# Two chained blocks on one core: the opening's vectors shared by two engines, one stream of modulation steps, sums of squares added up ahead

## The reference

```python
# first block, per layer l (mod = silu(c) @ ada_w[l] + ada_b[l], nine vectors of 1024)
n1 = rms_norm(h, norm_g[l, 0]) * (1 + sc1) + sh1
h = h + 0.5 * g1 * swiglu(n1, ...)          # F0 / F2
h = h + g2 * token_mixing(n2, ...)          # two attentions, gates, out
h = h + 0.5 * g3 * swiglu(n3, ...)          # F1 / F3
return rms_norm(h, final_g)
# second block, streams x and ctx (xc); per layer sh1, sc1, g1, sh2, sc2, g2 = silu(c) @ w_mod[i] + b_mod[i],
# and the same for c_ctx; layer 0 mixes by retention and gated linear scans, layer 1 by attention
yc, states = retention_gla_mixer(hc, ...)
y, _ = retention_gla_mixer(h, ..., states)
x = layer_norm(ALPHA * x + g1 * (y @ w_out), ...)
x = layer_norm(ALPHA * x + g2 * sq_relu_mlp(x * (1 + sc2) + sh2, w1, w2), ...)
```

## Time and profile before

| | us |
|---|---|
| median of 3 runs | 2336.91 (2334.52 to 2337.52) |
| profiled execution | 2339.74 |
| its span | 2338.0 |
| TensorE busy (matmul) | 2243.5 |
| VectorE, ScalarE, GpSimd busy | 1759.6, 1158.2, 109.5 |
| mean granted TensorE clock | 0.984 of full |

### The profile page before, as it was taken

One profiled execution on the slowest core, in us unless ns is written; L12 is line 12 of the kernel. 1 busy time (PEld: TensorE's weight loads), 2 busy tenths in 40 slices (PEclk: granted clock), 3 DMA queues, 4 the chain that ended last, 5 costly groups with the idle time before them and its releaser, 6 DMA issues.

```text
span 2338.0 us, 34014 instructions
## 1 busy us (share of the span) xinstructions
PE 2243.5 (96%) x14388; PEld 1960.2 (84%) x14404; DVE 1759.6 (75%) x2083; ACT 1158.2 (50%) x1445; POOL 109.5 (5%) x157
## 2 busy tenths in 40 slices
PE   7999999999999999999999889899989998999998
PEld 6888899888888888988888779778878887768886
DVE  3788776788888878678886666668788877676763
ACT  2544556555355445655534434447536633475742
POOL 1000000000000000000000000000000000000000
PEclk7999999999999999999999999999999999999999
DMA  6988664488878866448887426239788876304651
GB/s 242 311 278 305 228 198 145 148 298 291 307 228 276 306 223 210 140 145 291 288 305 246 137 80 204 100 109 293 261 278 276 269 277 225 109 19 140 203 197 55
DMA packets 330447, 505.24 MB, mean 216 GB/s; under 512 B 12327, under 2 KB 239878, under 8 KB 330295
## 3 DMA queue, kind: packets, MB, share of 16 engines
q1 hardware_dynamic: 288071, 340.70, 44.2%
q0 software_dynamic: 41616, 160.44, 19.7%
q10 hardware_dynamic: 608, 1.92, 0.2%
HBM read 501.98 MB, written 1.05 MB: 215 GB/s over the span
## 4 chain that ended last, share of the span: by engine, by line
PE 85%; DVE 9%; ACT 3%; issue 2%; DMA 1%; POOL 0%; ACTq 0%; DVEq 0%; SPq 0%; POOLq 0%
PE banks L577 35%; PE banks L578 18%; PE banks L569 7%; PE banks L571 7%; PE banks L570 7%; PE banks L796 2%; PE banks L743 2%; DVE wlo L1761 1%; PE banks L770 1%; PE banks L826 1%; PE banks L779 1%; PE banks L634 1%; DVE arena L1788 1%; DMA stage<-in_ffn_wu_dram 1%; DMA arena<-in_ada_w_dram 1%
## 5 line engine op out<-in xcount | busy, mean ns | idle before, releaser
L1761 DVE TENSOR_TENSOR wlo<-stage,whi 128x2048 fp32r<-128x2048 f32 (+1 forms) x326 | 737.1, 2262 | 184.2 <-ACT whi L1290 183.2
L1290 ACT CAST whi<-stage 128x2048 fp32r<-128x2048 f32 x322 | 615.0, 1911 | 387.7 <-PE banks L578 304.0
L577 PE MATMUL banks<-xs,whi 128*128 128x512 f32 x2176 | 768.0, 398 | 7.8 <-DVE xs L2008 4.3
L578 PE MATMUL banks<-xs,wlo 128*128 128x256 f32 x2176 | 609.5, 280 | 0.0
L577 PEld LDWEIGHTS banks<-xs,whi 128*128 128x128 f32 x2176 | 409.0, 188 | 109.0 <-issue 5.1
L569 PE MATMUL banks<-xs,whi 128*128 128x256 f32 x1440 | 416.5, 289 | 11.9 <-DVE xs L1952 7.9
L578 PEld LDWEIGHTS banks<-xs,wlo 128*128 128x128 f32 x2176 | 411.2, 189 | 0.1
L570 PE MATMUL banks<-xs,whi 128*128 128x256 f32 x1440 | 408.4, 284 | 0.0
L571 PE MATMUL banks<-xs,wlo 128*128 128x256 f32 x1440 | 408.3, 284 | 0.0
L577 PE MATMUL banks<-hidden_arena,whi 128*128 128x512 f32 x992 | 357.6, 402 | 1.1 <-DVE wlo L1761 1.1
L1788 DVE SCALAR_TENSOR_TENSOR arena<-modw,cact,arena 128x1024 f32<-128x1024 f32 x234 | 299.8, 1281 | 23.3 <-DMA modw<-in_w_mod_dram 15.7
(11 more groups left out here) (329 smaller groups left out, 2489.9 us busy)
## 6 DMA issues: line engine op xcount, KB each, us to landing
stage<-in_mlp_w_dram SPq DMA_DIRECT2D x96, 1024.0 KB, 5.4
modw<-in_w_mod_dram POOLq DMA_DIRECT2D x80, 1024.0 KB, 5.9
modw<-in_ada_w_dram POOLq DMA_DIRECT2D x66, 1024.0 KB, 5.5
stage<-in_ffn_wg_dram SPq DMA_DIRECT2D x44, 1024.0 KB, 5.7
stage<-in_ffn_wu_dram SPq DMA_DIRECT2D x44, 1024.0 KB, 7.3
stage<-in_ffn_wd_dram SPq DMA_DIRECT2D x44, 1024.0 KB, 7.4
stage<-in_ev_w_in_dram SPq DMA_DIRECT2D x24, 1024.0 KB, 5.4
stage<-in_w_in_dram SPq DMA_DIRECT2D x18, 1024.0 KB, 5.7
```

What stands on the lines that cost most here:

```text
L577: mm(out, hi, pair.rearrange("p a t -> p (a t)"), start=first_mm, stop=False, skip_group_check=True)
L578: return mm(out[:, 0:T], lo, pair[:, 0, :], start=False, stop=last_mm, skip_group_check=True)
L1290: nc.scalar.copy(whi[:, s, :], stage[:, s, :]).then_inc(hi_done, 1)
L1761: last = v.tensor_tensor(wlo[:, s, at], stage[:, s, at], whi[:, s, at].bitcast(F32), ALU.subtract)
```

## The change

It has five parts.

1. *Opening.* Of every quarter of the first scale and the first shift vector, VectorE takes the even half (`first_steps`: four steps a vector) and TensorE the odd half (`column_step`: eight one-column matmuls); `column_rest` adds VectorE's accumulator with eight more into the same column. No turn is left here. The first norm is done by rows: ScalarE squares x in rows with a running sum, VectorE multiplies the rows by the root, TensorE transposes them once more (`turn_rows("normal")`), and VectorE takes them from PSUM with the scale. The column sums n0 are gone. `keep_warm` calls of 4 or 2 stand between the groups.
2. *One stream of steps.* A vector may end in another phase than it began. Steps go into gate0 and gate1 (8 each), evoc and evox (4 each) and 4 more into evx; F1 and F3 have 32 for 40, Mc and M0 34 for 40. `ACC_ROOMS` holds five accumulators; a step waits only for the turn of the vector that last used its own. The vectors of the gate phases are turned at w = 1 of F1 and F3; in evc and evx a turn comes one chunk after the last step.
3. *Joined sums.* In evc and evx VectorE adds the 8 blocks up to one (`join`), and TensorE sums it in one matmul, for the squares of n6 and lc0 and the mean of lc0. Root and finish come one or two chunks later; in Mc and M0 the layer norm's pieces come one chunk later.
4. *Scan.* Three buffers for the query, the third in `xs`; `decays(u)` waits for the outputs of u - 3. The `keep_warm` calls inside the loop are gone, and two more memsets stand ahead of it.
5. The small transfers of evc are issued one load later.

```diff
-            "start": [ada(0, 1)],
             "F0": [ada(0, v) for v in range(2, 6)],
             "in0": [ada(0, 6), ada(0, 7)],
-            "F1": [ada(0, 8)] + [ada(1, v) for v in range(4)],
+            "gate0": [ada(0, 8)],
+            "F1": [ada(1, v) for v in range(4)],
             "F2": [ada(1, 4), ada(1, 5), wmod(0, 0, 2), wmod(0, 1, 2)],
             "in1": [ada(1, 6), ada(1, 7)],
-            "F3": [ada(1, 8), wmod(0, 2, 2)] + [wmod(0, v, 1) for v in range(3)],
-            "evc": [wmod(0, 3, 2), wmod(0, 4, 2)],
-            "evx": [wmod(0, 3, 1)],
-            "Mc": [wmod(0, 5, 2), wmod(0, 4, 1), wmod(0, 5, 1), wmod(1, 0, 2), wmod(1, 1, 2)],
-            "M0": [wmod(1, v, 1) for v in range(5)],
+            "gate1": [ada(1, 8)],
+            "F3": [wmod(0, 2, 2)] + [wmod(0, v, 1) for v in range(3)],
+            "evc": [wmod(0, 3, 2), wmod(0, 4, 2), wmod(0, 5, 2), wmod(0, 3, 1), wmod(0, 4, 1)],
+            "Mc": [wmod(0, 5, 1), wmod(1, 0, 2), wmod(1, 1, 2), wmod(1, 0, 1)],
+            "M0": [wmod(1, v, 1) for v in range(1, 5)],
...
+        gate_vectors = (mod_first["gate0"], mod_first["gate1"])
+        ACC_ROOMS = {"arena": arena[:, 43 * 256:47 * 256], "low": plain_rows[:, 0:1024], "mid": plain_rows[:, 1024:2048],
+                     "top": plain_rows[:, 2048:3072], "table": table[:]}
+
+        def acc_name(m):
+            if m in gate_vectors:
+                return "top"
+            if even0 <= m < even0 + 4:
+                return ("low", "mid")[(m - even0) % 2]
+            return "table" if m == even0 + 4 else "arena"
+
+        macc_of = lambda m: ACC_ROOMS[acc_name(m)]
+        acc_before = lambda m: max([a for a in range(m) if acc_name(a) == acc_name(m)], default=None)
+        first_acc = (ACC_ROOMS["arena"], hid[:].rearrange("p s f t -> p (s f t)")[:, 0:1024])
...
         STEPS = {
             "F0": [0] + 22 * [1] + 4 * [2] + [0, 0, 1, 1, 0, 0],
-            "F1": [0] + 4 * [1, 1, 1, 2] + 6 * [1] + 4 * [2] + [2, 0, 2, 2, 0, 0],
-            "Mc": [0] + 3 * [1, 1, 2, 1, 1] + [1, 0, 2, 2, 0, 2, 2, 2, 0, 2, 2, 0, 2, 2, 3, 0],
+            "in0": [2, 2, 2, 2, 0, 1, 1, 3, 3],
+            "gate0": [2, 1, 1, 1, 1, 1, 1],
+            "evc": [2, 2, 2, 0, 1, 1, 2, 2, 2, 2, 0, 0],
+            "evoc": [1, 2, 1, 0],
+            "evx": [1, 1, 0, 1, 1, 2, 0, 2, 2, 2, 0, 0],
+            "evox": [1, 2, 1, 0],
+            "Mc": [0] + 3 * [1, 1, 1, 1, 2] + [1, 0, 1, 2, 0, 2, 2, 2, 0, 2, 1, 0, 1, 2, 0, 0],
             "M1": [0, 0] + 8 * [1] + 22 * [0],
         }
-        for name, like in (("F2", "F0"), ("F3", "F1"), ("M0", "Mc")):
+        for name, like in (("F1", "F0"), ("F2", "F0"), ("F3", "F0"), ("in1", "in0"), ("gate1", "gate0"), ("M0", "Mc")):
...
+        turn_at["F1", 1], turn_at["F3", 1] = gate_vectors
+        EVEN_TURNS = {"c": {6: even0, 10: even0 + 1}, "x": {7: even0 + 2, 10: even0 + 3}}
...
-            "qd": [part(16 + 2 * i, 2) for i in range(2)],
+            "qd": [part(16, 2), part(18, 2), plain_xs[:, KB - 2:KB, :]],
...
-        EVEN_TURNS = {"c": (5, 9), "x": (9,)}
-        EVEN_STEPS = {"c": (1, 2, 2, 0, 2, 1, 2, 2, 2, 2, 0, 0), "x": (1, 1, 0, 1, 1, 0, 1, 1, 1, 1, 0, 0)}
+        JOIN_AT = {"c": 2, "x": 4}
...
-                if c == RING:
+                if c == RING + 1:
...
+            def column_step(i, q):
+
+                pe.wait_ge(start_landed[4 * i + q], 16)
+                t = 2 * q + 1
+                for k in range(KB):
+                    mm(first_column[i][:, k:k + 1], quarter(4 * i + q)[:, 1024 + k * P:1024 + (k + 1) * P], cact[:, 0, t:t + 1],
+                       start=q == 0 and k == 0, stop=False, skip_group_check=True)
+
+            def column_rest(i):
+
+                pe.wait_ge(first_step[i], 4)
+                for k in range(KB):
+                    last = mm(first_column[i][:, k:k + 1], first_acc[i][:, k * P:(k + 1) * P], ones[:, 0:1],
+                              start=False, stop=True, skip_group_check=True)
+                last.then_inc(pe_out.sem, pe_out.next(f"column{i}"))
+
             keep_warm(Y[:, 3, :], 12)
+            pe.wait_ge(act_out.sem, act_out.at("cact"))
+            column_step(0, 0)
+            keep_warm(R[:, 0, :], 4)
             turn_rows(0)
+            column_step(0, 1)
+            keep_warm(R[:, 0, :], 4)
             pe.wait_ge(param_landed, nparam)
             for k in range(KB):
                 transpose(R[:, 1, k * nwide:(k + 1) * nwide], wide_room[:, k * P:(k + 1) * P], nwide)
             transpose(R[:, 1, KB * nwide:KB * nwide + 7], narrow_room, 7).then_inc(pe_out.sem, pe_out.next("params"))
-            pe.wait_ge(act_out.sem, act_out.at("cact"))
-            turn_mod(0, R[:, 2:4, :])
-            rms_stat("n0")
+            for q in (2, 3):
+                column_step(0, q)
+                keep_warm(R[:, 0, :], 2)
+            column_rest(0)
+            pe.wait_ge(dve_out.sem, dve_out.at("rows"))
             pe.wait_ge(act_out.sem, act_out.at(("turned", 0)))
-            for t in range(8):
-                if t % 2 == 0:
-                    pe.wait_ge(start_landed[4 + t // 2], 16)
-                for k in range(KB):
-                    last = mm(Y[:, 0, k:k + 1], quarter(4 + t // 2)[:, (t % 2) * 1024 + k * P:(t % 2) * 1024 + (k + 1) * P],
-                              cact[:, 0, t:t + 1], start=t == 0 and k == 0, stop=t == 7, skip_group_check=True)
-            last.then_inc(pe_out.sem, pe_out.next("shift0"))
-            keep_warm(Y[:, 1, :], 12)
+            turn_rows("normal")
+            for q in range(4):
+                column_step(1, q)
+                keep_warm(R[:, 0, :], 2)
+            column_rest(1)
+            keep_warm(R[:, 0, :], 4)
...
-                    if which == "c" and c == 1:
-                        column_sums(other)
                     if which == "x" and c == 1:
-                        mean_sums(other, other_res)
-                    if which == "x" and c == 3:
-                        column_sums(other)
-                    if c == EVEN_TURNS[which][0]:
+                        pe.wait_ge(dve_out.sem, dve_out.at((other, "joined mean")))
+                        mm(stats_of(other)[3], ones, stats_of(other)[0][:, 0, :], start=True, stop=True) \
+                            .then_inc(pe_out.sem, pe_out.next((other, "mean")))
+                    if c == min(EVEN_TURNS[which]):
                         pe.wait_ge(dve_out.sem, dve_out.at((other, "rooted")))
                     if c in EVEN_TURNS[which]:
-                        turn_mod(mod_first["ev" + which] + EVEN_TURNS[which].index(c), Y[:, 2:4, :])
+                        turn_mod(EVEN_TURNS[which][c], Y[:, 2:4, :])
...
-                    if u < 3:
-                        keep_warm(R[:, 0, :], 3)
                     if u >= 1:
                         outputs(u - 1)
                     states(u)
...
+            def first_steps(i, q):
+
+                dve.wait_ge(start_landed[4 * i + q], 16)
+                w, cc = quarter(4 * i + q)[:, 0:1024], cact[:, 0, 2 * q:2 * q + 1]
+                if q == 0:
+                    v.tensor_scalar(first_acc[i], w, cc, None, ALU.mult).then_inc(first_step[i], 1)
+                else:
+                    dve.wait_ge(first_step[i], q)
+                    v.scalar_tensor_tensor(out=first_acc[i], in0=w, scalar=cc, in1=first_acc[i], op0=ALU.mult, op1=ALU.add) \
+                        .then_inc(first_step[i], 1)
...
+            for q in range(4):
+                first_steps(0, q)
+            dve.wait_ge(act_out.sem, act_out.at("rows"))
+            refine(row_rs, row_room, row_sum, D, 1e-6)
+            dve.wait_ge(pe_out.sem, pe_out.at(("turned", 0)))
+            for a in range(2):
+                last = v.tensor_scalar(xrows[:, a, :], xrows[:, a, :], row_rs[:, a:a + 1], None, ALU.mult)
+            done(last, "rows")
...
+                    mod_steps(STEPS[f"gate{l}"][g])
...
+            def join(key, signal_name, src):
+
+                room = stats_of(key)[0]
+                link(v.tensor_tensor(room[:, 0:4, :], src[:, 0:4, :], src[:, 4:8, :], ALU.add))
+                link(v.tensor_tensor(room[:, 0:2, :], room[:, 0:2, :], room[:, 2:4, :], ALU.add))
+                done(v.tensor_tensor(room[:, 0, :], room[:, 0, :], room[:, 1, :], ALU.add), (key, signal_name))
...
-                    if u >= 2:
-                        dve.wait_ge(pe_out.sem, pe_out.at(("o", which, u - 2)))
+                    if u >= 3:
+                        dve.wait_ge(pe_out.sem, pe_out.at(("o", which, u - 3)))
...
+            def first_shift():
+                first_steps(1, 2)
+                first_steps(1, 3)
+                conv(0)
+                first_vector(1)
+                done(v.memset(stat[:, 61:62], 0.0), "start_shift")
+
+            dve.wait_ge(pe_out.sem, pe_out.at(("turned", "normal")))
+            normal_split("n0", "F0", resx, lambda k: mc(("ada", 0, 0), k), first_shift)
```

155 lines of the change are left out of this document (84 added, 71 removed).

## The result

The changed kernel takes 2314.53 us, the median of four executions (2312.03 to 2318.83); the kernel before takes 2335.88 us, the median of four. The ratio is 0.9907, with a 95% interval of 0.9896 to 0.9919: faster by 21.4 us. The forecast was 2298, with a range of 2280 to 2314. The side is right, the gain is little more than half of the 38.7 us forecast, and the time lies just above the range. The profiled execution of the changed kernel took 2312.03 us for a span of 2310.2 us, 27.8 us less than the span before.

The account below looks back on a forecast made before the run. TensorE, busy in 96% of the span, was taken as the bound. Opening +1, ends of Mc and M0 -17.3, even projections -17.0 and scans -5.4 made -38.7: 2301.0 from the profiled 2339.7, 2298 by the median; range 2280 to 2314.

Parts of the forecast that it names:

- The second rival: Outside the opening: new waits eat half of the 39.7 us gain, giving 2318 us; chance 13%.
- if TensorE waits for the joined sums: evc and evx: a sign, named in advance, that the prediction is wrong; no size given.
- Ends of Mc and M0: Fewer steps behind the modulated input, no turn there in Mc, 0.5 us wait left in M0: -17.3 us.
- Even projections: Even mixer's projections, evc and evx: turns without waits and joined sums save 17.0 us (ends -10 and -18.3).
- up to 1.1, 0.8 taken: evx, joined sum at c = 4: TensorE's wait in us behind cast, low part and adds.
- each turn comes one chunk behind its last step: evc: the two turns no longer wait or run slowly, -7.2 us.
- Scans: -2.7 each: Both scans: three short waits and three warm-up groups on the chain go, together -5.4 us.
- Opening: +1: Opening: column work shared with TensorE, partly at the lower clock, costs net 1 us (ends -13.5 and +12).
- The fall near 23 us: Opening: TensorE's clock stays full to about 23 us, then runs at 1.2 GHz.
- the full-clock rival: Opening stays at full clock, 14.5 us further down, 2284 us; chance 22%.
- The third rival: Moved steps wait for their weight transfers; above 2.8 us unhidden each, slower than before; wholly unhidden 2381 us; chance 3%.
- the fourth: Rival: TensorE's turns move but wait as long, only removed matmuls pay: 2324 us; chance 4%.

Follow-up runs that it names:

- e4_three: Changed kernel with one Mc step moved a window later, evc's final norm and evx's join each moved ahead of a low part: 2294.11 us.
- s1_scans: e4_three with both scans put back as in the kernel before: 2301.5 us.
- a_again: The changed kernel itself, unedited, timed again: 2312.33 us.
- o2b_six: e4_three with six warm-up matmuls instead of two behind each of the opening's last six column quarters, repeated for a profile: 2289.79 us, single execution.

## Why the prediction was wrong

**The second rival came true in part.** It had 13% and said that each stage which loses a stall meets the next limit. It gave 2318; measured were 2314.5. It took half of the 39.7 us outside the opening away; in the profiled executions 22.8 of them came. The opening, 6 us better than forecast there, hid a part of the miss: that is luck and not the forecast's reasoning. The stages with the three new waits taken out come near the forecast's terms: Mc 9.7 us (2.4 and 7.3; forecast 8.8), evc 9.2 (5.1 and 4.1; 9.9), evx 5.0 (5.9), M0, which never had such a wait, 9.7 (8.5). The sizes of what was removed were about right. The step that failed is where the new order's waits were costed: 0 for Mc's turns, 0 for the norm in evc, 0.8 us for the join in evx. Taking them out gave 7.3, 4.1 and 7.4 us. The prediction had named one of these as a sign of being wrong, "if TensorE waits for the joined sums", and TensorE did.

**Ends of Mc and M0: "Mc has no turn there any more".** True and not enough. The count of steps was followed only behind the modulated input. With 34 steps in the new order Mc's fourth turn falls in window 23, the last whose turn lies in the banks of the second half, and its take-out falls in the next window behind the residual. M0 has the same table but begins at another step of a vector, its turn falls in window 22, and nothing waits. A term for the turns of the whole phase, with the banks of each, would have shown the wait: 5.42 us and 1.4 of slow matmuls.

**Even projections: a wait of "up to 1.1, 0.8 taken".** The join stands behind a cast, a low part and the adds, as the forecast had it; but ahead of the cast ScalarE does three activations from 1411.62 to 1414.83. They were in the trace of before, where nobody waited for them. The wait was 4.57 us, and with the slow matmuls behind it, for which the forecast had no term, the stage lost 7.4 us. For evc, "each turn comes one chunk behind its last step" left out that the final norm moved from c = 3 to c = 4, in front of that step: 2.31 us waited, 4.1 for the stage. The later turns also put the take-out of the last turn ahead of the scans, where TensorE now waits 1.4 us instead of 0.72 in each; that is still so in e4_three, and no run takes it out.

**Scans: -2.7 each.** Another term that was too large. Measured 1.1 and 0.7 against before, and 1.6 each by undoing. Units 1 to 2 and 2 to 3 came 0.55 and 1.05 us closer, units 3 to 4 and 5 to 6 not at all, which is the pattern forecast. But the first wait grew by 0.82 us (2.10 to 2.92), for the memsets (in s1_scans, without them, the longest wait is 2.2 again), and the matmuls removed had mostly filled waits.

**Opening: +1, found -5.0.** The fall near 23 us was right, 0.53 at 24 to 28, and the full-clock rival (22%) is out for this kernel. (One reading of the trace was loose and cost nothing: before, TensorE did not stand idle from 13.0 to 23.9 us, since 25 transposes of 2.75 us lie in between the earlier trace rows.) Three parts were off. The column groups at 34.12 and 36.42 took 2.01 and 2.07 us instead of 3.4, which the scheme had no place for: 2.8 us, in some executions only. The FFN's first matmul stood 1.5 us behind the column and not 4: before, the last twelve warm-up matmuls took 4.41 us from 53.61 on and stood between, now the last four take 1.87. And the wait at 72.77 was 2.11 us without the clock falling behind it. In a_again, where the first and the third of these fail, 0.7 us of gain is left at the end of F0. So most of what made up for the missed terms elsewhere came with that one execution.

**What held.** In both profiled openings of the changed kernel the clock fell to 0.50 with TensorE busy 4.00 of 4.00 us, mostly in one-column work, and in the kernel before it stood at 0.50 from 36 to 52 us, where TensorE was busy throughout with one-column matmuls alone. The page of the Trainium skill "TensorE: Matmul & The Clock Gate", section Why this matters for your kernels, advises leaving no long idle gaps between bursts of matmuls, so that throughput doesn't drop. These rows show that this alone doesn't keep the clock up: there was no gap, and it fell. The same page of the Trainium skill (Part 4: PE-mode transpose) says that transposes don't count as busy in the same way. No run here settles that: in the changed kernel the clock, if it rose, rose while or just after the sixteen transposes of 30.67 ran; in o2b_six it rose near 31, ahead of the transposes at 32.32. Moved steps did not wait for their weights: in gate0, 313 to 391 us, the eight new steps show 0.0 us idle ahead of them. Mc had one such wait, the 1.96 us above. The third rival is out, and so is the fourth, since the turns' waits fell from 17.2 to 2.3 us.

## What to carry to other kernels

When a stall is removed, follow every wait of the new order through its stage, not only at the place of the old one: which banks a result lies in, who takes it out, and what stands ahead of that on the same engine. In-order engines lose most where work that is ready stands behind work that waits; moving the norm and the join ahead of a waiting low part, and one step by one window, gave nearly as much again as the whole change (18 to 20 us beside 21.4). And where executions differ by 3 to 5 us in one stage, read an edit from its own stage in the timeline, since the median mixes it with the others.
